# A trunk layer with its MLP on one core: another prologue, and another order at the begin of the first MLP product

## The chip, the cores and the metric

The kernel runs on one core of a Trainium2 chip, as one program. The metric is the device time of one execution in microseconds (us). A core has engines that run their own instruction queues side by side and meet only at semaphores: PE multiplies matrices, DVE and ACT work on vectors, GpSimd (POOL in the profile) too, and SP issues the DMA transfers.

## The reference, cut to what matters

One layer of a trunk over 1024 tokens of width 1024, with a context of 256 tokens:

```
m = silu(c) @ w_mod + b_mod                  # six vectors: sh1, sc1, g1, sh2, sc2, g2 (the context has two)
h = rmsnorm(x, norm1_w) * (1 + sc1) + sh1    # likewise hc of the context
proj = h @ w_in                              # q, k, v, gates, and the inputs of a short conv and a pool
mix = concat(gla(proj), conv(proj), pool(proj)) @ w_out
x = x + g1 * mix
h2 = rmsnorm(x, norm2_w) * (1 + sc2) + sh2
x = x + g2 * (square(relu(h2 @ w_mlp1)) @ w_mlp2)      # width 4096 between the two
return rmsnorm(x, final_norm_w)
```

All inputs and the output are fp32.

## The kernel before

Tensors stand transposed, 128 features to a partition block (k = 0 to 7), tokens along the free axis. A factor is split into a high part (rounded to the matrix engine's format) and a low part (what the rounding left), and a product is the sum of three: high x high, high x low, low x high. ACT makes high parts with a copy, DVE low parts with a subtraction. PE sums in PSUM, in the tiles `main`, `ob` and `sm`. Each engine's queue is written out by hand, one function per engine, and semaphores order them.

**Prologue** (to the first `gate_products`). SP loads the context, eight pieces of x, and the modulation weights `wmod` in four pieces of 2 MB, with the gate weights and the first weight tile between. ACT squares each piece over 1280 columns (1024 tokens and 256 of the context) into two accumulators and two passing buffers; DVE adds them up (`SQ_ADDED`), PE sums over the partitions, and ACT takes logarithm and exponential for the root, in two halves of the columns. `modulation_rows(j)` (L1000) multiplies one piece of `wmod` by the two vectors, eight k in `GROUPS` column groups of PE; ACT copies the rows out (`copy_rows`, L1478); `modulation_turned(j)` (L1011) turns them into columns and adds the groups up with `fold`; DVE makes shift and scale of them (`modulation`). For each k DVE scales x, ACT writes the high part, DVE the low part (`low1`, L2079). PE runs `gate_part(k)` and `value_part(k)` (L1194) on them. Before the first comes everything of pieces 0 and 1, and `low1` waits for a product of rows. `keep_busy` puts idle products of PE in the first microseconds.

**MLP1** (`h2 @ w_mlp1`). The 32 column tiles are taken in 16 pairs. Pairs 0 and 1 are plain products. From pair 2 on, the two tiles and two halves of the tokens make a 2 x 2 block product in seven products instead of eight (12 matmuls each, in the order `HID_ORDER`), for which sums of blocks are needed. Per pair:

- GpSimd makes four sums of weight blocks (`part_sums1`, L885 to L893);
- ACT makes seven high parts of weights (`w1_high`, L1826), DVE the low ones (`w1_low`, L2458);
- PE's seven products (L1382) accumulate in three banks; ACT copies them out of PSUM into `hid` (`copy_out`, L1885), DVE adds the rest (`add_out`, L2520; `third_out`), and ACT makes relu and square of the blocks (`first_out`, `next_out`, `last_block`);
- for the second MLP product the squared blocks are prepared in seven parts: DVE makes four sums (`t_made`, L2492 to L2506), ACT the high parts (`t_high`, L1880), DVE the low ones (`t_low`, L2513), all in the order `T_ORDER`, and SP stores them (`keep_hidden`, L695).

So the parts of pair i-1 are made while PE multiplies pair i. Before its copies ACT waits until all seven parts of the pair before are made (`act.wait_ge(t_lo, prev * NPART)`), since `hid` has two places. PE's products wait for the copies and sums of the pair before, whose banks they reuse (`y_copied`, `y_added`). Pairs 2 to 15 run as `period(i, ...)`, in a loop for most; the begin, with the parts of pairs 0 and 1 and pair 2, is written out. SP loads the weights for pair i+2 (`load_w1`) in the middle of the stores of pair i-1.

## Time and profile before

| | us |
|---|---|
| median of 3 runs | 1088.19 |
| lowest, highest | 1086.53, 1090.26 |
| the profiled execution | 1089.87 |
| its span, from the first to the last instruction | 1088.0 |
| PE busy | 1062.0 |
| DVE busy | 826.6 |
| ACT busy | 508.9 |
| GpSimd busy | 307.9 |

The profile is one execution. It lists the busy time of each engine, what each idle stretch ended with (the releaser), and the clock granted to PE, as a share of its full speed. Overlapping matmuls are recorded with a duration longer than their distance in time: two records of 0.39 may start 0.23 apart. The same holds for small vector instructions, of which each drains while the next starts.

### The profile page before, as it was taken

Reading aid. Unit: us, or ns where it says so; the run is one execution under the profiler, and the core shown is the slowest. Engines: PE = TensorE matmul, PEld = TensorE weight load, DVE = VectorE, ACT = ScalarE, POOL = GpSimd, SP = SyncE. Lnnn points to the kernel's source line nnn. Section 1 sums busy time; section 2 is a strip of 40 time slices with the busy share of each in tenths; the row PEclk is TensorE's granted clock in tenths of the full one; section 3 lists DMA queues with packets and bytes.
Section 4 is the critical chain, followed back from the end, with each engine's and each line's share of the span. In section 5 each row is a group of like instructions: output and inputs, shape, how many; then the busy total and the mean of one; then the engine's idle time right before and its main releaser. Section 6 shows DMA issues by size and latency. Waiting matters only on the chain.

```text
span 1088.0 us, 16279 instructions
## 1 busy us (share of the span) xinstructions
PE 1062.0 (98%) x5512; PEld 851.8 (78%) x5512; DVE 826.6 (76%) x1070; ACT 508.9 (47%) x818; POOL 307.9 (28%) x280
## 2 busy tenths in 40 slices
PE   8999999999999999998999999999999999999995
PEld 4578888777778888787888888888778888888884
DVE  4887869737544987799878787787987777777776
ACT  5657533356624312576666666666422222222234
POOL 1000006287301344013232323323333122222322
PEclk9999999999999999999999999999999999999998
DMA  9523240011013555225857566667746844864604
GB/s 369 225 97 116 89 142 31 31 40 40 21 40 136 231 191 216 78 78 227 315 229 273 232 257 245 239 262 284 295 168 259 334 185 184 339 253 185 256 1 155
DMA packets 58900, 199.80 MB, mean 184 GB/s; under 512 B 5600, under 2 KB 6880, under 8 KB 58336
## 3 DMA queue, kind: packets, MB, share of 16 engines
q1 hardware_dynamic: 58848, 199.11, 48.3%
q8 instruction: 33, 0.54, 0.2%
q14 instruction: 19, 0.16, 0.1%
HBM read 139.32 MB, written 59.77 MB: 183 GB/s over the span
## 4 chain that ended last, share of the span: by engine, by line
PE 49%; DVE 4%; issue 1%; POOL 0%; DVEq 0%; ACT 0%; ACTq 0%; POOLq 0%
PE ob L1382 13%; PE main L1424 13%; PE sm L1382 10%; PE sm L1424 8%; PE ob L1424 5%; DVE XR L2632 1%; DVE XR L2699 1%; DVE slot L2463 1%; DVE stage L2513 1%; DVE slot L2458 0%; DVE stage_last L2513 0%; DVE t_tmp L2497 0%; DVE t_tmp L2506 0%; DVE hid L2520 0%; DVE hid L2499 0%
## 5 line engine op out<-in xcount | busy, mean ns | idle before, releaser
L953 PE MATMUL main<-a_hi,w_hi 128*128 128x512 f32 x376 | 125.8, 416 | 0.0
L1382 PE MATMUL ob<-h_sum,slot 128*128 128x512 f32 x504 | 122.8, 393 | 3.0 <-DVE hid L2520 3.0
L1838 ACT ACTIVATE slot<-raw 128x512 fp32r<-128x512 f32 x80 | 50.2, 631 | 153.1 <-PE main L1424 58.4
L953 PE MATMUL main<-a_lo,w_hi 128*128 128x512 f32 x376 | 116.7, 391 | 0.0
L953 PE MATMUL main<-a_hi,w_lo 128*128 128x512 f32 x376 | 116.2, 390 | 0.0
L1382 PEld LDWEIGHTS ob<-h_sum,slot 128*128 128x128 f32 x504 | 95.7, 190 | 23.4 <-issue 3.4
L2632 DVE SCALAR_TENSOR_TENSOR XR<-main,mods,XR 128x512 f32<-128x512 f32 x112 | 83.3, 748 | 28.8 <-PE main L1424 27.7
L953 PEld LDWEIGHTS main<-a_hi,w_lo 128*128 128x128 f32 x376 | 70.6, 188 | 15.6
L953 PEld LDWEIGHTS main<-a_lo,w_hi 128*128 128x128 f32 x376 | 70.6, 188 | 15.6
L953 PEld LDWEIGHTS main<-a_hi,w_hi 128*128 128x128 f32 x376 | 66.7, 188 | 17.9 <-issue 5.8
L1424 PE MATMUL main<-t_even,slot 128*128 128x512 f32 x336 | 78.1, 389 | 0.0
L2458 DVE TENSOR_TENSOR slot<-raw,slot 128x512 fp32r<-128x512 f32 x70 | 62.5, 895 | 18.5 <-ACT slot L1826 18.5
L1382 PE MATMUL sm<-h_hi,slot 128*128 128x512 f32 x224 | 73.5, 389 | 0.0
L1424 PEld LDWEIGHTS main<-t_even,slot 128*128 128x128 f32 x336 | 63.1, 188 | 13.1
L824 POOL TENSOR_TENSOR scaled_state<-tst,decay 64x128 f32<-64x128 f32 x60 | 29.0, 483 | 151.2 <-ACT tst L1579 146.7
L2463 DVE TENSOR_TENSOR slot<-raw,slot 128x512 fp32r<-128x512 f32 x80 | 61.3, 782 | 0.2 <-ACT slot L1838 0.2
L2632 DVE SCALAR_TENSOR_TENSOR XR<-sm,mods,XR 128x512 f32<-128x512 f32 x64 | 47.7, 748 | 13.3 <-PE sm L1424 12.4
L885 POOL TENSOR_TENSOR held<-raw 128x512 f32<-128x512 f32 x14 | 24.8, 1774 | 109.7 <-DMA raw<-wstream 59.8
L914 POOL TENSOR_TENSOR raw<-part_sum,raw 128x512 f32<-128x512 f32 x16 | 21.0, 1313 | 122.3 <-DVE slot L2463 122.3
L2632 DVE SCALAR_TENSOR_TENSOR XR<-ob,mods,XR 128x512 f32<-128x512 f32 x48 | 35.8, 750 | 18.4 <-PE ob L1424 18.3
L893 POOL TENSOR_TENSOR held<-raw 128x512 f32<-128x512 f32 x14 | 23.4, 1672 | 90.9 <-DVE slot L2458 90.9
L1424 PE MATMUL main<-stage,slot 128*128 128x512 f32 x168 | 47.4, 391 | 1.5 <-DVE XR L2632 0.7
(354 smaller groups left out, 2453.7 us busy)
## 6 DMA issues: line engine op xcount, KB each, us to landing
hidden_kept<-stage SPq DMA_DIRECT2D x98, 512.0 KB, 4.2
raw<-wstream SPq DMA_DIRECT2D x60, 512.0 KB, 4.3
t_even<-hidden_kept SPq DMA_DIRECT2D x56, 512.0 KB, 5.8
raw<-wstream SPq DMA_DIRECT2D x16, 1024.0 KB, 5.2
stage<-hidden_kept SPq DMA_DIRECT2D x21, 512.0 KB, 5.4
stage_last<-hidden_kept SPq DMA_DIRECT2D x21, 512.0 KB, 6.1
wmod<-wm SPq DMA_DIRECT2D x4, 2048.0 KB, 23.6
mbuf<-wm SPq DMA_DIRECT2D x16, 512.0 KB, 4.0
```

Of the source, the lines that this page charges most:

```text
L824: pool.tensor_tensor(scaled_state[DK:P, :], tst[DK:P, h % 2, c, :], decay[DK:P, h, c:c + 1].broadcast_to([DK, DV]), ALU.mult).then_inc(sta ...
L885: pool.tensor_tensor(sums, a21, a22, ALU.add).then_inc(w1_sum, 1)
L893: pool.tensor_tensor(sums, a12, a11, ALU.subtract).then_inc(w1_sum, 1)
L914: pool.tensor_tensor(a11, sums, a11, ALU.subtract).then_inc(w2_sum, 1)
L953: ins = pe.matmul(main[:, bank, half * HALF:(half + 1) * HALF], w[:, slot, k, :], x[:, half * HALF:(half + 1) * HALF], start=begin, stop=end)
L1382: ins = pe.matmul(hid_bank(acc, odd), slots1[j][:, w, kp, :], parts[x][:, kp, :], start=PARTS[j][3] and kp == 0 and m == 0, stop=kp == KP ...
L1424: ins = pe.matmul(product_bank(s, acc, q), slots2[j][:, w, q, kp, :], tset[odd][j][kp][:, x, :], start=begins and kp == 0 and n == 0, stop ...
L1838: act.activation(slots2[j][:, 0, :, :, :], operand(s, j), ACT.Copy).then_inc(w2_hi, 1)
L2458: tt(slots1[j][:, 1, :, :], operand1(b, j), slots1[j][:, 0, :, :].bitcast(F32), ALU.subtract).then_inc(w1_lo, 1)
L2463: tt(slots2[j][:, 1, :, :, :], operand(s, j), slots2[j][:, 0, :, :, :].bitcast(F32), ALU.subtract).then_inc(w2_lo, 1)
L2513: tt(y[:, 1, :], sources(odd)[j], y[:, 0, :].bitcast(F32), ALU.subtract).then_inc(t_lo, 1)
L2632: stt(out=XR[m][:, cols], in0=product_bank(s, acc, q), scalar=mods[:, 3, m:m + 1], in1=XR[m][:, cols], op0=ALU.mult, op1=ALU.add).then_inc ...
```

## The change

**Prologue.** Each square has a buffer of its own (`square_place`), over the 1024 tokens; the squares of the context are taken once for all k and summed apart. DVE joins only squares 2 and 3, 4 and 5, and, by halves, 6 and 7. `wmod` comes in eight pieces of 1 MB, piece k when square k has been taken (they lie over the buffers of later tiles), and the rows products have 256 columns in four column groups. Modulation is done per k with two small instructions of DVE. The context is scaled early, in two instructions. Products of rows and turns for k = 2 to 7 stand between the gate and value products; the gate's high products stand ahead of its low ones. The idle products are 10 instead of 18 at the start, and two between rows(1) and turned(1).

**MLP1.** `T_ORDER` changes for all pairs but the last. In the begin, a copy out of PSUM waits for its own block's part and sum (`block_free`) instead of all seven parts of the pair before. The parts of pairs 0 to 3 stand behind weight blocks of pairs 2 to 5, in an order written out for ACT and DVE; period 5 has the rest. The part sums of pairs 2 and 3 go from GpSimd to DVE. SP loads the weights of pair 4, 5 and 6 with `load_next`, pair 4 ahead of the stores of pair 0.

The diff, cut to its core; the written orders of ACT and DVE are shown for pair 2:

```diff
-T_ORDER = (0, 3, 1, 2, 5, 4, 6)
+T_ORDER = (0, 3, 4, 1, 2, 5, 6)
 T_AT = {j: n for n, j in enumerate(T_ORDER)}
+LAST_AT = {j: n for n, j in enumerate((0, 3, 1, 2, 5, 4, 6))}
+def t_at(pair):
+    return LAST_AT if isinstance(pair, int) and pair == NMP - 1 else T_AT
...
-GROUPS = 3
+GROUPS = 4
 ROWS = 32 * GROUPS
-SHIFTED_FIRST = 3
-FILL = (18, 2)
-SQ_ADDED = (1, 2, 3, 5, 6)
-COPY_AT = {0: 1, 2: 2, 4: 3}
+FILL = (10, 2)
...
-        wmod = [at(f"wmod{j}", [P, KT, HALF], F32, HA + place * KIB) for j, place in enumerate((0, 32, 16, 48))]
+        wmod = [at(f"wmod{j}", [P, KT, 2 * P], F32, HA + (j % 2 * 32 + j // 2 * 8) * KIB) for j in range(KT)]
...
-        sq1 = at("sq1", [P, 2, NA], F32, ZA + 8 * KIB)
-        acc1 = at("acc1", [P, NA], F32, ZA + 28 * KIB)
+        squares1 = at("squares1", [P, 6, N], F32, ZA + 8 * KIB)
+        squares1_late = at("squares1_late", [P, 2, N], F32, ZT)
+        squares_c = at("squares_c", [P, KT, NC], F32, ZT + 8 * KIB)
...
             def load_wmod(j):
-                sp.dma_start(wmod[j][:, :, :].rearrange("p k c -> p (k c)"), wm1[j]).then_inc(wmod_loaded[j], 16)
+                sp.wait_ge(sq1_made, j + 1)
+                sp.dma_start(wmod[j][:, :, :], wm1[j // 2].rearrange("p (k j c) -> p k j c", j=2, c=2 * P)[:, :, j % 2, :]
+                             ).then_inc(x_wmod_loaded[j], 16)
...
             load_wmod(0)
             sp.dma_start(wg[:, :, :].rearrange("p k c -> p (k c)"), wg_in).then_inc(wg_loaded, 16)
+            load_wmod(1)
             load_tile(0)
-            load_wmod(1)
-            load_wmod(2)
-            load_wmod(3)
+            for j in range(2, KT):
+                load_wmod(j)
...
+            def load_next(i, load):
+                sp.wait_ge(w1_lo, i * NPART - NPART)
+                load()
+            load_next(2, lambda: load_w1(4, 0, stream1(4)))
             for j in T_ORDER:
                 keep_hidden(0, j)
+            for i in (3, 4):
+                for j in T_ORDER:
+                    keep_hidden(i - 2, j)
+                load_next(i, lambda: load_w1(i + 2, i % 2, stream1(i + 2)))
+            for j in T_ORDER:
...
-            part_sums1(2, 0, first=True)
-            part_sums1(3, 1)
...
-                    ins = pe.matmul(sm[32 * g:32 * g + 32, s % 2, :], silu_wide[:, k, :], wmod[j][:, k, :],
+                    ins = pe.matmul(sm[32 * g:32 * g + 32, s % 2, 0:2 * P], silu_wide[:, k, :], wmod[j][:, k, :],
...
-                for q in range(4):
+                for q in range(2):
...
+            pe.wait_ge(squares_c_added, 2)
+            for q in range(2):
+                ins = pe.matmul(ob[:, HALF:HALF + NC], ones, squares_c[:, q, :], start=q == 0, stop=q == 1)
+            ins.then_inc(sums_c_done, 1)
+            for ready, k in (((sq1_made, 1), 0), ((sq1_made, 2), 1), ((acc1_made, 1), 2), ((acc1_made, 2), 4)):
+                pe.wait_ge(*ready)
+                sums_of(square_place(k), (1, 0), k == 0, False)
+            for n, half in enumerate((1, 0)):
+                pe.wait_ge(acc1_made, 3 + n)
+                sums_of(square_place(7), (half,), False, True).then_inc(sums1_done, 1)
             modulation_rows(0)
             modulation_turned(0)
             modulation_rows(1)
+            keep_busy(FILL[1])
...
             gate_part(0)
+            modulation_rows(2)
             value_part(0)
-            modulation_rows(2)
-            gate_part(1)
             modulation_turned(2)
-            value_part(1)
-            modulation_rows(3)
-            gate_part(2)
-            value_part(2)
-            modulation_turned(3)
-            for k in range(3, KT):
+            for k in range(1, KT - 1):
+                if k + 2 < KT:
+                    modulation_rows(k + 2)
                 gate_part(k)
-                if k >= 4:
-                    value_part(k - 1)
+                if k + 2 < KT:
+                    modulation_turned(k + 2)
+                value_part(k)
+            gate_part(KT - 1)
             value_part(KT - 1)
...
-                act.wait_ge(x_loaded[k], 16)
-                if k in SQ_ADDED[2:] + (KT - 1,):
-                    act.wait_ge(acc1_made, sq_place(k) - 1)
-                act.activation(SUM_FIRST[k][:, :] if k in SUM_FIRST else sq1[:, sq_place(k) % 2, :], xs[:, k, :],
-                               ACT.Square).then_inc(sq1_made, 1)
+                act.activation(mrow[:, j % 2, :], sm[0:ROWS, s % 2, 0:2 * P], ACT.Copy).then_inc(small_free[s % 2], 1)
+            act.activation(squares_c[:, :, :], xs[:, :, N:NA], ACT.Square).then_inc(squares_c_made, 1)
...
+                act.activation(square_place(k), xs[:, k, 0:N], ACT.Square).then_inc(sq1_made, 1)
+                if k == 2:
+                    act.wait_ge(sums_c_done, 1)
+                    log1(slice(N, NA), ob[:, HALF:HALF + NC])
+                    act.wait_ge(rs1_made, 1)
+                    root1(slice(N, NA))
...
+                if k + 2 < KT:
+                    copy_rows(k + 2)
...
+            def modulation(k):
+                s = S_OF[("turn", k)]
                 dve.wait_ge(small_done, s + 1)
-                for q in range(2):
-                    i = 2 * j + q
-                    ts(ab1[:, i, 0:2], sm[:, s % 2, 4 * q:4 * q + 2], one_col("bmod", i), None, ALU.add)
-                    ins = ts(ab1[:, i, 2:4], sm[:, s % 2, 4 * q + 2:4 * q + 4], one_col("bmod", KT + i), 1.0, ALU.add, ALU.add)
-                ins.then_inc(small_free[s % 2], 1)
-                dve.wait_ge(*small_freed(s))
-                ts(ab1[:, 2 * j, 2:4], ab1[:, 2 * j, 2:4], one_col("n1", 2 * j), None, ALU.mult)
-                ts(ab1[:, 2 * j + 1, 2:4], ab1[:, 2 * j + 1, 2:4], one_col("n1", 2 * j + 1), None, ALU.mult).then_inc(ab_made, 1)
-                dve.wait_ge(ab_made, j + 1)
-            for n, k in enumerate(SQ_ADDED):
-                dve.wait_ge(sq1_made, k + 1)
-                acc = acc1 if k < 4 else acc1b
-                tt(acc[:, :], acc[:, :], sq1[:, n % 2, :], ALU.add).then_inc(acc1_made, 1)
-                dve.wait_ge(acc1_made, n + 1)
+                ts(ab1[:, k, 2:4], sm[:, s % 2, 2:4], mods[:, 0, k:k + 1], one_col("n1", k), ALU.add, ALU.mult)
+                ts(ab1[:, k, 0:2], sm[:, s % 2, 0:2], one_col("bmod", k), None, ALU.add).then_inc(small_free[s % 2], 1)
+                dve.wait_ge(*ab_ready(k))
...
+            dve.wait_ge(sq1_made, 4)
+            tt(square_place(2), square_place(2), square_place(3), ALU.add).then_inc(acc1_made, 1)
+            dve.wait_ge(rs1_made, 2)
+            scale_context(0)
+            dve.wait_ge(sq1_made, 6)
+            tt(square_place(4), square_place(4), square_place(5), ALU.add).then_inc(acc1_made, 1)
+            dve.wait_ge(sq1_made, 8)
+            for half in (1, 0):
+                cols = slice(half * HALF, (half + 1) * HALF)
+                tt(square_place(7)[:, cols], square_place(7)[:, cols], square_place(6)[:, cols], ALU.add).then_inc(acc1_made, 1)
+            scale_context(1)
...
+            for k in range(1, KT):
+                modulation(k)
+                scale1(k)
+                if k == 1:
+                    weight_low(0)
+                if k < 3:
+                    low1(k)
+                elif k > 3:
+                    low1(k - 1)
...
+            def block_free(pair, j, sums=0):
+                if sums:
+                    act.wait_ge(t_sum, pair * 4 + sums)
+                act.wait_ge(t_lo, pair * NPART + (T_AT[j] + 1))
...
             t_high(0, 0, 0, "first")
+            t_high(0, 0, 3, "first")
             w1_high(2, 0, 0, True)
             w1_high(2, 1, 0, True)
             plain_hidden(1, 0)
-            t_high(0, 0, 3, "first")
-            t_high(0, 0, 1, "first")
             w1_high(2, 2, 0, True)
-            t_high(0, 0, 2, "first")
             w1_high(2, 3, 0, True)
+            w1_high(2, 4, 0, True)
+            block_free(0, 0, 1)
+            copy_out(2, 0, 0, ACC_A, 0, 0, 0)
             plain_hidden(1, 1)
-            act.wait_ge(t_sum, 1)
-            act.wait_ge(t_lo, T_AT[0] + 1)
-            copy_out(2, 0, 0, ACC_A, 0, 0, 0)
-            w1_high(2, 4, 0, True)
-            t_high(0, 0, 5, "first")
-            t_high(0, 0, 4, "first")
-            t_high(0, 0, 6, "first")
             w1_high(2, 5, 0, True)
             w1_high(2, 6, 0, True)
-            for j in T_ORDER[:2]:
-                t_high(1, 1, j, "plain")
+            t_high(0, 0, 4, "first")
+            block_free(0, 4)
+            copy_out(2, 0, 1, ACC_A, 2, 0, 1)
+            t_high(0, 0, 1, "first")
+            t_high(0, 0, 2, "first")
+            copy_out(2, 0, 2, ACC_C, 3, 1, 1)
+            w1_high(3, 0, 1)
+            w1_high(3, 1, 1)
             first_out(2, 0)
-            act.wait_ge(t_lo, NPART)
-            copy_out(2, 0, 1, ACC_A, 2, 0, 1)
-            copy_out(2, 0, 2, ACC_C, 3, 1, 1)
+            t_high(0, 0, 5, "first")
+            next_out(2, 0)
+            t_high(0, 0, 6, "first")
...
+            def part_sums1(pair, b, steps):
+                v, sums = pair - 2, held[:, :, :]
+                a11, a12, a21, a22 = quarter1(b, 0, 0), quarter1(b, 0, 1), quarter1(b, 1, 0), quarter1(b, 1, 1)
+                for step in steps:
+                    if step == 0:
+                        dve.wait_ge(w1_loaded[b], pair * 16 + 16 * b)
+                        if v > 0:
+                            dve.wait_ge(w1_lo, v * NPART + (HID_AT[3] + 1 - NPART))
+                        ins = tt(sums, a21, a22, ALU.add)
+                    elif step == 1:
+                        dve.wait_ge(w1_sum, v * 4 + 1)
+                        ins = tt(a21, a11, a21, ALU.subtract)
+                    elif step == 2:
+                        dve.wait_ge(w1_sum, v * 4 + 2)
+                        dve.wait_ge(w1_lo, v * NPART + (HID_AT[0] + 1))
+                        ins = tt(a11, sums, a11, ALU.subtract)
+                    else:
+                        dve.wait_ge(w1_sum, v * 4 + 3)
+                        dve.wait_ge(w1_lo, v * NPART + (HID_AT[1] + 1))
+                        ins = tt(sums, a12, a11, ALU.subtract)
+                    ins.then_inc(w1_sum, 1)
...
+            part_sums1(2, 0, (0, 1))
+            w1_low(2, 0, 0)
+            part_sums1(2, 0, (2,))
+            w1_low(2, 1, 0)
+            t_made(0, 0, 1, "first")
             t_low(0, 0, 0)
-            w1_low(2, 0, 0)
-            w1_low(2, 1, 0)
+            w1_low(2, 2, 0)
+            w1_low(2, 3, 0)
             dve.wait_ge(sum_made, 13)
             sum_low(2)
+            part_sums1(2, 0, (3,))
+            w1_low(2, 4, 0)
+            t_made(0, 0, 2, "first")
+            t_made(0, 0, 3, "first")
             t_low(0, 0, 3)
-            t_low(0, 0, 1)
-            w1_low(2, 2, 0)
-            t_low(0, 0, 2)
-            w1_low(2, 3, 0)
-            t_made(0, 0, 4, "first")
-            w1_low(2, 4, 0)
-            t_low(0, 0, 5)
-            add_out(2, 0, 0, ACC_B, 1, 0, 0)
             t_low(0, 0, 4)
-            t_low(0, 0, 6)
             sum_low(3)
             w1_low(2, 5, 0)
-            for j in T_ORDER[:2]:
-                t_low(1, 1, j)
             w1_low(2, 6, 0)
-            for n in (1, 2, 3):
-                t_made(1, 1, n, "plain")
+            add_out(2, 0, 0, ACC_B, 1, 0, 0)
+            t_low(0, 0, 1)
+            t_low(0, 0, 2)
+            add_out(2, 0, 1, ACC_A, 4, 1, 1)
+            part_sums1(3, 1, (0, 1))
+            w1_low(3, 0, 1)
+            t_made(0, 0, 4, "first")
+            part_sums1(3, 1, (2,))
+            w1_low(3, 1, 1)
+            t_low(0, 0, 5)
+            t_low(0, 0, 6)
+            third_out(2, 0)
...
+                if kind == "fifth":
+                    t_low(prev, old, 0)
+                    t_low(prev, old, 3)
                 for n in (1, 2, 3):
                     t_made(prev, old, n)
                 w1_low(i, 3, odd)
-                t_low(prev, old, 1)
+                t_low(prev, old, 4)
                 add_out(i, odd, 0, ACC_B, 1, 0, 0)
                 w1_low(i, 4, odd)
+                t_low(prev, old, 1)
+                w1_low(i, 5, odd)
                 t_low(prev, old, 2)
...
+            period(5, 1, "fifth")
+            with dve.Fori(3, 7) as q:
```

## Rows read from the trace of the kernel before

**Rows 1.** The page: busy time, share of the span and instructions of each engine.

```profile
PE 1062.0 (98%) x5512; PEld 851.8 (78%) x5512; DVE 826.6 (76%) x1070; ACT 508.9 (47%) x818; POOL 307.9 (28%) x280
```

**Rows 2.** Waits of PE: line, releaser: us in total, times, longest.

```profile
PE ob L1382 <- DVE hid L2520: 3.0, 1, 3.0
```

**Rows 3.** Windows: length; busy (x) PE, PEld, DVE, ACT, POOL; clock; DMA; GB/s.

```profile
25.00:50.00 25.00, 22.95 (x129) 11.26 (x124) 21.20 (x41) 16.59 (x24) 1.51 (x3) 0.93 0.68 283
```

**Rows 4.** Timeline of ACT, squares and the last root: start, us, engine, line, operation.

```profile
9.24 1.27 ACT L1485 ACTIVATE acc<-xs 128x1280 f32<-128x1280 f32 x1 [5.79 <-DMA xs<-xt]
...
18.62 1.27 ACT L1485 ACTIVATE sq<-xs 128x1280 f32<-128x1280 f32 x1 [0.50 <-DVE acc1b L2069]
...
25.53 0.63 ACT L1499 ACTIVATE rs<-rs 128x512 f32<-128x512 f32 x1
```

**Rows 5.** Timeline of PE and DVE to the first gate product and after.

```profile
29.70 4.10 PE L1000 MATMUL sm<-wmod,silu_wide 128*32 128x512 f32 x16 [0.58 <-DMA wmod<-wm]
...
33.89 1.23 DVE L2079 TENSOR_TENSOR a_lo<-sq,a_hi 128x1024 fp32r<-128x1024 f32 x1 [2.57 <-PE sm L1000]
...
35.60 0.65 PE L1194 MATMUL main<-a_hi,wg_parts 128*64 128x512 f32 x2
...
38.61 2.77 PE L1000 MATMUL sm<-wmod,silu_wide 128*32 128x512 f32 x16
...
42.51 0.95 PE L1011 MATMUL sm<-fold,mrow 96*128 96x2 f32 x8
```

**Rows 6.** Timeline of DVE and PE at the end of the prologue.

```profile
63.70 1.22 DVE L2139 CAST zsb<-main 32x1024 fp32r<-32x1024 f32 x1 [0.79 <-PE ob L1196]
...
67.18 0.36 PE L1183 MATMUL ob<-zsb,gw_parts 128*128 128x256 f32 x1
```

**Rows 7.** Windows of 2 us: context loading, then pieces of 2 MB.

```profile
4.00:6.00 2.00, 2.00 (x5) 1.20 (x4) 1.20 (x6) 0.00 (x0) 0.60 (x2) 1.00 1.06 374
...
24.00:26.00 2.00, 2.00 (x14) 0.48 (x14) 0.97 (x2) 1.94 (x4) 1.86 (x3) 1.00 1.06 453
```

**Rows 8.** Timeline of PE, pair 2 of MLP1 and its end.

```profile
492.76 0.39 PE L1382 MATMUL ob<-h_hi,slot 128*128 128x512 f32 x1
...
500.92 2.88 PE L1382 MATMUL sm<-h_sum,slot 128*128 128x512 f32 x12
...
512.24 4.58 PE L1382 MATMUL ob<-h_sum,slot 128*128 128x512 f32 x12 [3.00 <-DVE hid L2520]
...
516.66 0.39 PE L1382 MATMUL ob<-h_hi,slot 128*128 128x512 f32 x1
```

**Rows 9.** Window of the late product and the next.

```profile
512.00:516.00 4.00, 3.76 (x10) 2.99 (x11) 4.00 (x6) 2.63 (x5) 1.60 (x1) 0.57 0.66 255
```

**Rows 10.** Timeline of DVE at the begin of MLP1.

```profile
482.56 2.29 DVE L2469 TENSOR_TENSOR h_sum<-h_raw,h_sum 128x2048 fp32r<-128x2048 f32 x1
...
484.76 0.69 DVE L2492 TENSOR_TENSOR t_tmp<-hid 128x512 f32<-128x512 f32 x1
...
504.41 1.28 DVE L2513 TENSOR_TENSOR stage<-hid,stage 128x512 fp32r<-128x512 f32 x2
...
511.42 0.67 DVE L2520 TENSOR_TENSOR hid<-hid,ob 128x512 f32<-128x512 f32 x1
...
513.22 2.37 DVE L2513 TENSOR_TENSOR stage<-hid,stage 128x512 fp32r<-128x512 f32 x2
```

**Rows 11.** Timeline of ACT and GpSimd there.

```profile
488.26 0.62 ACT L1880 ACTIVATE stage<-hid 128x512 fp32r<-128x512 f32 x1
...
504.63 3.42 POOL L885 TENSOR_TENSOR held<-raw 128x512 f32<-128x512 f32 x1 [5.90 <-DVE slot L2458]
...
512.84 1.60 POOL L890 TENSOR_TENSOR raw<-held,raw 128x512 f32<-128x512 f32 x1 [3.10 <-DVE slot L2458]
```

**Rows 12.** Timeline of DVE in a later pair.

```profile
541.44 0.69 DVE L2520 TENSOR_TENSOR hid<-hid,sm 128x512 f32<-128x512 f32 x1 [0.37 <-PE sm L1382]
...
547.93 1.64 DVE L2458 TENSOR_TENSOR slot<-raw,slot 128x512 fp32r<-128x512 f32 x1 [1.43 <-ACT slot L1826]
```

More of the change, by code:

```diff
@@ L186 @@
 BANKED = ("vt", "kt", "kc", "cs", "u", "A", "ns", "pl", "md")
-SMALL = [(_name, _j) for _j in range(KT // 2) for _name in ("rows", "turn")]
+SMALL = [(_name, _j) for _j in range(KT) for _name in ("rows", "turn")]
 for _t in range(NPROJ):
@@ L1017, in keep_busy @@
                 for _ in range(count):
[L1018 removed]
+                    pe.matmul(main[:, 0, 0:NFIRST], ones, small[:, 0:NFIRST], start=True, stop=True)
             pe.wait_ge(small_in_done, 16)
@@ L1022, in _, with sums_of @@
             pe.wait_ge(c_ready, 1)
-            def sums_of(squares, halves, with_context, first, last):
+            def sums_of(squares, halves, first, last):
                 for half in halves:
@@ L1187, in gate_products, with first_product_of @@
                 ins.then_inc(tile_done, 1)
-            def first_product_of(k, m, rows, parts):
+            def first_product_of(k, m, rows, parts, first=True, last=True):
                 for n, (w, x, c) in enumerate(parts):
-                    begin, end = k == 0 and n == 0, k == KT - 1 and n == len(parts) - 1
+                    begin, end = first and k == 0 and n == 0, last and k == KT - 1 and n == len(parts) - 1
                     for half in range(2):
@@ L1956, in period @@
                 w1_high(i, 5, odd)
-                t_high(prev, old, 4)
+                t_high(prev, old, 5)
                 copy_out(i, odd, 2, ACC_C, 3, 1, 1)
@@ new lines, in _ @@
+            third_out(3, 1)
+            w1_low(4, 1, 0)
+            w1_low(4, 2, 0)
+            t_low(2, 0, 1)
+            t_low(2, 0, 2)
+            w1_low(4, 3, 0)
+            t_made(2, 0, 4)
+            t_low(2, 0, 5)
+            add_out(4, 0, 0, ACC_B, 1, 0, 0)
+            w1_low(4, 4, 0)
+            t_low(2, 0, 6)
+            t_made(3, 1, 1)
+            t_low(3, 1, 0)
+            t_low(3, 1, 3)
+            w1_low(4, 5, 0)
+            t_made(3, 1, 2)
+            t_made(3, 1, 3)
@@ L2581, in period @@
+            t_low(3, 1, 4)
+            w1_low(4, 6, 0)
+            t_low(3, 1, 1)
+            add_out(4, 0, 1, ACC_A, 4, 1, 1)
+            w1_low(5, 0, 1)
+            t_low(3, 1, 2)
+            t_made(3, 1, 4)
+            third_out(4, 0)
+            w1_low(5, 1, 1)
+            t_low(3, 1, 5)
+            t_low(3, 1, 6)
             def period(i, odd, kind=""):
```

325 lines of the change are left out of this document (178 added, 147 removed).

## The prediction, made before the changed kernel ran

> **What bounds the kernel now.** I read the page's busy times first: the matrix engine (PE) is busy 1062.0 of the 1088.0 us span [rows 1], so what the change can give back is the other 26 us and the stretches at the lower clock. The list of PE's waits comes next. Its longest entry after the first load is one stall of 3.0 us behind DVE's sum `hid` (L2520) [rows 2], the place that the second half of the change rewrites. The windows of 25 us then show the one other weak stretch, the prologue: from 25 to 50 us PE is busy 22.95 of 25 and its clock is granted 0.93 [rows 3]. Then I went through the timeline of both stretches. Nearly everything behind each of them is PE's own queue, so a microsecond won or lost there should reach the end of the kernel.
>
> **The prologue, before.** Eight squares of 1280 columns take ACT from 9.24 to 19.89 (18.62 + 1.27), each waiting for a 512 KB piece of x or for DVE; then sums, logarithms, and the last root, done at 26.16 [rows 4]. But the first gate product starts only at 35.60, because `a_lo` waits (2.57 us) for the second product of modulation rows, which itself waited 0.58 us for its 2 MB of `wmod` and ran 4.10 instead of 2.77 us [rows 5]. From 35.60 to `gate_products` at 67.18 [rows 6] are 31.6 us.
>
> **The prologue, after.** *Squares.* With a buffer for each square ACT waits only for x. I let the last piece land near 18.0: the first square starts at 9.24, and seven further pieces at the 374 GB/s of 4 to 6 us [rows 7] would take 9.8 us, but the old last square, which waited 0.50 for DVE [rows 4], puts the last one at 18.1 or before. Its square over 1024 columns takes 1.0 to 1.1 (1.27 x 0.8), DVE adds two halves, 0.6 each (1.23 for 1024 columns [rows 5], halved), PE sums two halves (0.9 each, estimated as half of four recorded matmuls), done at 21.1 and 22.0. Logarithm and root per half (about 0.65 each with the root's 0.63 [rows 4]) end at 23.9 instead of 26.16.
>
> *First gate product.* Rows(0) now has 256 columns in four column groups instead of 512 in three. The trace holds no such product: half of 2.77 [rows 5] is 1.39 if groups do not help, and 1.04 if they share in proportion (3/4). I take 1.1, nearer the second, since the parts of one product in the trace overlap already. A turn falls from 8 recorded matmuls in 0.95 [rows 5] to four, 0.45. So: rows(0) at 22.0, turn at 23.8 (it waits for the copy on DVE), rows(1) at 24.3, two fillers 1.4, turn(1) at 26.7, gate(0) at 27.2. That is 8.4 us ahead of 35.60.
>
> *The loop.* Six rows products and turns that stood before 35.60, or beside it, now stand between the gate and value products: 6 x (1.1 + 0.45) = 9.3. The eight gate and value parts: 2.72 us for 12 matmuls of 512 columns [rows 8] is 0.23 each, half that for 256, so gate 4 x 0.23 + 2 x 0.12 = 1.16, value 6 x 0.23 + 3 x 0.12 = 1.74, together 8 x 2.9 = 23.2. DVE has some 3.0 us per k (scale 1.2, low part 1.2, context 0.34, small ones 0.26) beside PE's 4.5, ACT 2.5, so both are covered; I add 1.2 for the first two k, where they are not ahead yet. 27.2 + 23.2 + 9.3 + 1.2 = 60.9 is the end of the last value product. The copies for the gates start 1.7 before (59.2) and take 3.3 (before: 63.70 to 67.18, 3.48, of it some on PE's last word [rows 6]): `gate_products` at 62.5, 4.7 us before the old 67.18. PE then stands 1.6 us, and a stall of 3 us cost clock in this trace [rows 9]; I leave 0.5 for that: **-4.2 us**.
>
> *Bounds.* The eight 1 MB pieces of `wmod` are read in runs of 1 KB. The context, in such runs too, moves at 374 GB/s at the start, where the 2 MB pieces later move at 453 [rows 7]; I took 353, a little under the low one, so that a piece lands every 3 us, with the gate weights and the first weight tile between at 21, 24, 29, 32, 35, 38, 41 and 44 us, each ahead of its product. At 294 GB/s `gate_products` comes at 65.0, and at 252 at 67.7, past the old. Rows products of 1.39 instead of 1.1 give 64.5. At the upper rate and 1.0 us a product it is 61.6. So -5.6 to about 0, the value nearer the good end. The Trainium skill (DMA: Bandwidth & Descriptors, the specification table) puts the full line rate at transfers from 512 B up; by that rule the 1 KB runs would cost nothing, and an estimate with it is 0.3 us earlier. The slower windows stand at the start of the kernel, so they do not decide it.
>
> **MLP1's begin, before.** PE starts pair 2 at 492.76, three products later is at 500.92 (2.72 each), and so is due for the seventh at 509.08; it starts it at 512.24 and the next at 516.66 [rows 8]. 3.16 us late, and 4.42 - 2.72 = 1.70 more in a product that ran at a granted clock of 0.57 [rows 9]: the old loss is **4.86 us**. The cause is DVE's queue, full from 484.76 until the sum at 511.42 [rows 10].
>
> **MLP1's begin, after.** The freed copies let ACT go ahead, and the parts of the plain pairs are spread behind the weight blocks. But DVE does no less: it takes over eight part sums from GpSimd (pairs 2 and 3), and the work that was crowded before 512 is moved to pairs 3, 4 and 5. So I ask when DVE reaches the last sum that PE needs before the steady state, add_out(5,1). From 484.77 to it, in the order written out, DVE has 106 instructions:
> 101 of 128x512 (28 weight low parts, 34 hidden low parts, 20 sums for parts, 11 add_out, 8 part sums). Two in a row take 1.28 with 0.68 for one [rows 10], a pitch of 0.60: 60.6.
> 2 low parts of 128x2048 at 2.20 (482.56 to 484.76 [rows 10]) and 3 third_out at 0.64: 6.3.
> GpSimd: an instruction of DVE beside one of GpSimd takes longer. Two hidden low parts took 2.37 at 513.22, 1.28 at 504.41 [rows 10], beside a GpSimd sum of 1.60 [rows 11]: 1.09 held. In the new order GpSimd still does pairs 4, 5 and 6, ten sums in this stretch: 9 x 1.1 + 0.3 = 10.2. Add_out has an operand in PSUM and stayed at 0.67 and 0.69 [rows 10, 12], so I charge it nothing.
> Waits of DVE for ACT and PE, by adding ACT's queue at 0.62 for a copy [rows 11] beside it: 2.6 before the first weight block, since ACT must first make t_high(0,3), at 488.26 before as well; 1.6 in the rest of pair 2, 0.9 for PE's fifth product, 1.5 in pair 3, 1.5 in pair 4, 2.6 in pair 5, 1.1 for DVE's own semaphores: 11.8.
> Sum 88.9: add_out(5,1) is done at 573.7. PE is due there after 27 products, at 492.76 + 27 x 2.72 = 566.2. PE is late by 7.5 us in all, in pieces: about 1.9 in pair 3, 0.8 and 1.7 in pair 4, 0.7, 1.5 and 1.0 in pair 5. The old piece of 3.16 is gone, and what is late next is the same queue, one to three pairs later. No piece reaches 3 us, so I take no loss of clock. One sum of GpSimd in the old trace, 3.42 long instead of 1.60 [rows 11], waited itself instead of holding DVE; one of the ten so gives 0.5 back: **7.0, against 4.86: +2.1 us.**
> *Bounds.* The holds decide. Without any, DVE's work is 10.2 shorter, its waits for ACT grow in the place of most of that slack, and what stays late is 0.8: -4.1. At 1.2 a hold it is 8.6: +3.8. The queue of SP costs nothing: the load for pair 4 is moved ahead of the stores, and its buffer is free as early as before; the seven stores that now stand behind it free places of parts that ACT needs one pair later.
> By the Trainium skill (SBUF — State Buffer, "SBUF: two separate sides"), an instruction of DVE with two SBUF inputs and one of GpSimd that reads SBUF exclude each other for the whole instruction. The trace agrees in kind, since add_out with its PSUM operand is not held, and not in size: 1.09 of 1.60.
>
> **The sum.** -4.2 + 2.1 = -2.1. The profiled execution took 1089.87 (span 1088.0 and 1.87 around it) and would take 1087.8; it lies 1.68 above the median of 1088.19, against which the forecast is **1086.1**.
>
> **The rivals.**
> *B, the stalls vanish.* DVE's instructions and GpSimd's fall into each other's gaps: in the steady pairs before, one of four sums held DVE (547.93, 1.64 [rows 12]). With two of ten holds the late sum is 1.5 or less: -3.4, and with -4.2: 1080.6. For it speaks that DVE now has less crowding at any one time; against it, that DVE stays nearly without idle time to 574.
> *C, the prologue gives less than it says.* Rows products cost 1.39 or the pieces of `wmod` come late, so `gate_products` is at 64.5: -2.7, and with +2.1 the time is 1087.6. For it: the product that followed late data ran 4.10 [rows 5]. Against: the pieces are half as large and the first one is asked for a good 8 us before its use.
> *D, slower: the holds recur in every pair.* In the steady state after pair 5 DVE has 22 instructions, 13.2 us, in a pair of 19.04 (7 x 2.72), and four sums of GpSimd beside them. At 1.1 a hold that is 17.6 at most, and the pair fits with a few tenths left once waits are counted. From about 1.3 a hold it does not, and each of the ten pairs 6 to 15 pays: at 1.4 it is 0.7 a pair, 7.3, and 12.8 at the begin, +7.9 + 7.3 - 4.2 = +11; just past the point +5, so 1093 to 1099, and I take 1093 as its time. For it: the order inside the periods is changed, so the gaps that GpSimd found before [rows 12] are not the same. Against: no hold of one instruction above 1.1 in the trace. The skill's rule above, with its whole instruction (1.60), would bring this case for certain: an estimate by it is 17 us at the begin and 1.5 a pair.
>
> **How the numbers follow.** Forecast 0.50, with its own range of 1083.5 to 1089; B 0.28; C 0.10; D 0.12. A measurement of this kernel can tell about 0.3%, 3.3 us, from no change: the border is at 1084.9 and 1091.5. Faster: B's 0.28 and 0.14 of the forecast's 0.50 make 0.42. Same: 0.36 and C's 0.10 make 0.46. Slower: D, 0.12. The range goes from B's time with the prologue's bound less one, 1079.5, to 1091.5, short of D.
>
> **What would show it.** Right: `gate_products` near 62.5 with the first gate product near 27; no PE stall near 512, and several of 0.7 to 2 us between 525 and 575, released by DVE or ACT; DVE without idle time there, with instructions of 1.6 to 1.7 beside GpSimd's. Wrong: rows products over 1.3 us or waits for `wmod`; PE without stalls from 520 to 575; or a wait for L2520 or L1885 in every later pair.

## The result, and the profile after

The changed kernel takes 1091.16 us (median of 20 runs, 1089.54 to 1092.85) against 1088.1 for the kernel before, taken beside it: 1.0026 times as long, with a 95% interval of 1.0020 to 1.0033. I had forecast 1086.1, two microseconds faster. The time lies inside the range, but on the other side of no change. The profiled execution took 1092.85 (span 1091.1), the slowest of the 20.

The prologue did nearly what was forecast. Timeline of PE in the changed kernel (columns as in [rows 5, 6]):

```profile
24.45 1.07 PE L1016 MATMUL sm<-wmod,silu_wide 128*32 128x256 f32 x16
...
27.16 0.65 PE L1210 MATMUL main<-a_hi,wg_parts 128*64 128x512 f32 x2
...
63.14 0.36 PE L1199 MATMUL ob<-zsb,gw_parts 128*128 128x256 f32 x1 [1.80 <-DVE zsb L2229]
```

A product of rows takes 1.07 (forecast 1.1), the first gate product starts at 27.16 (27.2; before 35.60), `gate_products` at 63.14 (62.5; before 67.18): 4.04 us earlier. But PE stood 1.80 us ahead of it, and behind it the clock fell. Windows of the changed kernel (columns as in [rows 3]):

```profile
62.00:64.00 2.00, 0.86 (x5) 0.81 (x6) 0.75 (x3) 1.50 (x3) 0.00 (x0) 1.00 1.02 377
64.00:66.00 2.00, 2.00 (x14) 2.00 (x13) 2.00 (x3) 0.30 (x1) 0.00 (x0) 0.66 0.55 211
66.00:68.00 2.00, 2.00 (x11) 2.00 (x10) 1.61 (x2) 1.91 (x3) 0.00 (x0) 0.50 0.27 59
...
475.00:500.00 25.00, 25.00 (x112) 20.70 (x111) 20.94 (x24) 17.55 (x22) 0.00 (x0) 1.00 0.23 85
500.00:525.00 25.00, 25.00 (x112) 20.72 (x111) 22.85 (x35) 17.67 (x32) 3.31 (x2) 1.00 0.77 294
525.00:550.00 25.00, 21.64 (x88) 17.10 (x86) 22.84 (x32) 14.47 (x26) 6.63 (x4) 0.93 0.65 234
550.00:575.00 25.00, 22.19 (x94) 17.47 (x95) 22.32 (x29) 16.26 (x30) 7.97 (x5) 1.00 0.86 318
```

The first product of pair 2 starts at 490.20, only 2.56 us earlier than before [rows 8]: 1.5 went to the half clock (the lower of 1.2 and 2.4 GHz) between 64 and 68. The lower four windows are MLP1's begin. PE, whose loss at 500 to 525 was 3 us before, is full there now, and loses 3.4 and 2.8 us in the two windows behind it. Timeline of PE in the changed kernel, the late products and the ones that follow:

```profile
490.20 0.39 PE L1405 MATMUL ob<-h_hi,slot 128*128 128x512 f32 x1
...
527.73 4.48 PE L1405 MATMUL ob<-h_sum,slot 128*128 128x512 f32 x12 [2.01 <-DVE hid L2629]
...
532.01 0.51 PE L1405 MATMUL ob<-h_hi,slot 128*128 128x512 f32 x1
...
550.12 2.97 PE L1405 MATMUL ob<-h_sum,slot 128*128 128x512 f32 x12 [1.48 <-DVE hid L2629]
...
561.89 3.01 PE L1405 MATMUL sm<-h_sum,slot 128*128 128x512 f32 x12 [0.64 <-DVE slot L2544]
...
566.15 3.04 PE L1405 MATMUL ob<-h_sum,slot 128*128 128x512 f32 x12 [1.25 <-ACT hid L1914]
...
572.70 3.00 PE L1405 MATMUL ob<-h_sum,slot 128*128 128x512 f32 x12 [0.80 <-DVE hid L2629]
...
575.54 0.39 PE L1405 MATMUL ob<-h_hi,slot 128*128 128x512 f32 x1
```

575.54 is the first product of pair 6, 28 products after 490.20; at 2.72 each it would be at 566.36. So 9.2 us are lost (before: 4.86): 6.2 are the waits in brackets, 1.6 the product at 527.73, which took 4.28 instead of 2.72 at the lower clock, the rest some tenths after each wait. The waits stand where the forecast put them, and DVE is what is late. Its own waits, from 482 to 573 us (line, releaser: us, times, longest):

```profile
DVE slot L2544 <- ACT slot L1855: 5.4, 5, 1.8
DVE stage L2622 <- ACT stage L1909: 3.3, 5, 1.2
DVE held L2555 <- DMA raw<-wstream: 0.7, 1, 0.7
DVE hid L2629 <- PE ob L1405: 0.7, 1, 0.7
```

These are 10.1 us (forecast 11.8). The kernel before had no such wait from 484 to 512. Of these waits 4.6 us lie before 512. And where GpSimd begins its sums, DVE is held, so that its instruction ends only after GpSimd's (timeline of GpSimd and DVE):

```profile
521.03 1.68 POOL L903 TENSOR_TENSOR held<-raw 128x512 f32<-128x512 f32 x1 [98.22 <-DVE slot L2544]
521.47 1.79 DVE L2544 TENSOR_TENSOR slot<-raw,slot 128x512 fp32r<-128x512 f32 x1
...
523.18 1.78 DVE L2622 TENSOR_TENSOR stage<-hid,stage 128x512 fp32r<-128x512 f32 x1
```

1.79 instead of 0.69, the hold of 1.1 that I had read from [rows 10, 11]. Of the ten sums of GpSimd from 521 to 573 us nine held DVE so. The Trainium skill (SBUF — State Buffer, "SBUF: two separate sides") lets the one that starts first keep the other out for its whole instruction. The sum of 1.68 was 0.44 us old when DVE's instruction began, so 1.24 of it were left, against a hold of 1.1: the trace agrees with the rule in size too, to 0.14 us. The prediction had denied that, since it compared the hold with the whole 1.60.

At the end the kernel loses another 0.9 us: from ACT's last instruction to the end of the span it is 6.6, before 5.6 (below).

### The profile page after: what moved, and what is told of

Same layout as the page of the kernel before. It is cut to its first block, busy times and chain, and to the rows that moved or that the text cites. A ratio compares the mean times of both kernels' runs of the same rounds, so it can differ in the third digit from the quotient of the medians.

```text
span 1091.1 us, 16343 instructions
## 1 busy us (share of the span) xinstructions
PE 1059.0 (97%) x5566; PEld 851.3 (78%) x5566; DVE 845.1 (77%) x1070; ACT 511.9 (47%) x827; POOL 297.0 (27%) x272
## 4 chain that ended last, share of the span: by engine, by line
PE 75%; DVE 12%; issue 4%; ACT 4%; POOL 3%; DMA 1%; DVEq 0%; SPq 0%; ACTq 0%; POOLq 0%
PE main L969 17%; PE main L1447 13%; PE ob L1405 11%; PE sm L1447 8%; PE sm L1405 7%; PE ob L1447 6%; PE main L987 2%; PE main L1338 2%; DVE stage L2622 1%; POOL scaled_state L843 1%; POOL tst L846 1%; PE main L1210 1%; PE main L1371 1%; PE ob L1371 1%; PE ob L1003 1%
## 5 line engine op out<-in xcount | busy, mean ns | idle before, releaser
L903 POOL TENSOR_TENSOR held<-raw 128x512 f32<-128x512 f32 x12 | 20.1, 1672 | 142.3 <-DVE slot L2544 142.3
L1405 PEld LDWEIGHTS sm<-h_hi,slot 128*128 128x128 f32 x224 | 42.0, 188 | 8.7
```

The costliest lines, as they stand in the source:

```text
L1405: ins = pe.matmul(hid_bank(acc, odd), slots1[j][:, w, kp, :], parts[x][:, kp, :], start=PARTS[j][3] and kp == 0 and m == 0, stop=kp == KP ...
```

## The experiments

Each ran beside the kernel before; the ratio is to its runs, with the 95% interval. MLP1 is the stretch from the first product of pair 2 to the first of the second MLP product, in the profile: 271.8 us before, 276.5 in the changed kernel.

**1 and 2: each half alone.** No edit but leaving out the other half's.

> The changed prologue with the MLP1 of the kernel before. Theory (clock): gate_products comes 4.0 us earlier, but PE stands 1.8 us before it and the matmuls behind it run at half clock for 1.5 us more; net -2.5, so 1085.6 against 1088.1. Rival (the loss of 3 us is in the prologue: later tiles lose what the prologue won): 1088 to 1091. What I had forecast for this part: -4.2, 1083.9.

1085.38 us, 0.9985 (0.9976 to 0.9994), against 1087.67 for the kernel before beside it: the time that the theory gave, but its reason is not in the profile, so that the agreement is in part luck. `gate_products` comes at 63.17 after the same stall, and the clock does not fall, neither there nor at the old stall of 3.0 us in MLP1:

```profile
508.33 2.99 PE L1392 MATMUL ob<-h_sum,slot 128*128 128x512 f32 x12 [2.99 <-DVE hid L2540]
511.16 0.39 PE L1392 MATMUL ob<-h_hi,slot 128*128 128x512 f32 x1
```

The product behind the stall takes 2.83 us here; in [rows 8] it took 4.42.

> The prologue of the kernel before with the changed MLP1. Theory: the begin of MLP1 loses 9.2 us instead of 4.9, and the change to MLP2 0.4 more: +4.7, so 1092.8 against 1088.1. Rival (the two halves disturb each other, MLP1 alone is as forecast): +2.1, 1090.2. Rival (the end of the kernel, where the profiled execution shows 0.9 us more from the last instruction to the last store, is part of the change): +5.6, 1093.7.

1092.56 us, 1.0040 (1.0027 to 1.0054), 4.9 above the same 1087.67: the whole loss, and more, is MLP1's. The rival with the end does not hold, since the end is 5.6 us here, as in the kernel before. The clock stays at 1.00 behind the longest stall:

```profile
530.53 2.97 PE L1395 MATMUL ob<-h_sum,slot 128*128 128x512 f32 x12 [1.87 <-DVE hid L2609]
533.34 0.39 PE L1395 MATMUL ob<-h_hi,slot 128*128 128x512 f32 x1
```

MLP1 takes 275.0 us against 270.7 in experiment 1: 4.3 us longer with no fall of the clock in either. Its begin loses 7.7 us (pair 6 starts at 576.85, 28 products after 493.00) against 3.8.

**3: is it the clock?**

```diff
             value_part(KT - 1)
+            pe.wait_ge(*ab_ready(KT - 1))
+            for _ in range(2):
+                pe.matmul(sm[:, 0, 0:NFIRST], ones, small[:, 0:NFIRST], start=True, stop=True)
             gate_products(0)
...
                     if j == 6:
+                        if nth == 2:
+                            pe.wait_ge(plain_relu, 4)
+                            for _ in range(2):
+                                pe.matmul(main[:, 0, 0:NFIRST], ones, small[:, 0:NFIRST], start=True, stop=True)
```

> The changed kernel, with two idle products of PE ahead of gate_products and two ahead of the wait of the last product of pair 3; no other work changes. Theory (clock): PE no longer stands 1.80 and 2.17 us there, the clock stays at 1.00, and 1.5 + 1.6 us come back: 1088.1 against 1091.2. Rival (the slow products are due to something else, weight loads or PSUM): 1091.2, or up to 0.5 slower where an idle product ends after the wait.

1090.57 us, 1.0030 (1.0018 to 1.0042): not what the theory said. In its profile the clock stays at 1.00 in both places, the two waits are 0.6 and 0.7, and that execution (1090.0) is 2.9 below the profiled one of the changed kernel. But the medians do not differ: the changed kernel's profile had been its slowest execution, and three of the six runs here have a mean clock of 0.994 as well. Of ten profiles with the 1.8 us stall unfilled, three show the fall behind it. So the clock's price in a profile is a draw, and it does not explain the 3 us. It may hold a part of them: the mean clock is 0.9946 over the 20 runs of the changed kernel and 0.9954 over 68 of the kernel before, and 0.0008 of 1090 us is 0.9 us, an estimate of the most that this can be.

**4: are the holds real?** GpSimd's sums shortened:

```diff
-                sums = held[:, :, :]
+                cut = lambda a: a[:, 0:1, 0:1]
+                a11, a12, a21, a22, sums = cut(a11), cut(a12), cut(a21), cut(a22), cut(held[:, :, :])
```

> The changed kernel with the part sums of GpSimd (pairs 4 to 15) cut to one column of 512, so that GpSimd hardly holds DVE; these sums are left out of the computation. Theory (holds): the ten holds of 1.1 us before add_out(5,1) go, the late pieces of pairs 3 to 5 shrink from 9.2 us to 1 or 2, and the kernel takes 1083 to 1084. Rival (DVE's eight added sums and the waits for ACT in the written order make it late, not the holds): 1089 to 1091.

1083.62 us, 0.9966 (0.9953 to 0.9979): 7.5 below the changed kernel, as the holds ask. The short sums are also ready earlier, which this run can't tell from the holds; experiment 5 leaves nothing out. All that is left of PE's waits from 484 to 760 us, in MLP1 and at the step to the second product:

```profile
PE sm L1406 <- DVE slot L2545: 0.6, 1, 0.6
PE main L1448 <- DVE stage_last L2623: 0.6, 1, 0.6
PE ob L1406 <- ACT hid L1915: 0.2, 1, 0.2
```

**5: all sums on DVE in the changed kernel.** `part_sums1` of pairs 4 to 15 in DVE's periods (steps 0 to 2 behind `w1_low(i + 1, 0)`, step 3 behind `w1_low(i, 3)`), none on GpSimd.

> The changed kernel with the part sums of all pairs on DVE, none on GpSimd; nothing is left out. Theory (holds): up to add_out(5,1) DVE gets ten more instructions of 0.60 (6.0 us) and loses the holds of 10.2, so PE is late by about 4.0 instead of 6.7 us: 1088.4 against 1091.2. Rival (DVE's own work is what counts, and holds hide in its waits): ten instructions later, 1094 to 1097, and a wait in every later pair.

1086.53 us, 0.9985 (0.9976 to 0.9994): 4.6 below the changed kernel, more than I said. MLP1 takes 271.9. Four more instructions of DVE in a pair (2.4 us) cost less than four of GpSimd beside it. Without any hold the changed order is still 3.2 us behind the old one (experiment 6).

**6, 8 and 11: the old order, with the sums on DVE.** The changed prologue, the order of MLP1 before, and (11: for pairs 2 and 3 only, GpSimd the rest):

```diff
             sum_low(1)
+            part_sums1(2, 0, (0, 1))
             for n in (1, 2, 3):
                 t_made(0, 0, n, "first")
             t_low(0, 0, 0)
             w1_low(2, 0, 0)
+            part_sums1(2, 0, (2,))
...
             w1_low(2, 3, 0)
+            part_sums1(2, 0, (3,))
...
             w1_low(3, 0, 1)
+            part_sums1(3, 1, (0, 1))
...
             w1_low(3, 1, 1)
+            part_sums1(3, 1, (2,))
```

> The changed prologue, the order of MLP1 of the kernel before, and the part sums of all pairs on DVE (four of pair 2 before the late sum, those of pair 3 behind it). Theory (holds): before add_out(2,1) six holds of 1.1 go (6.4 us) and four instructions of 0.60 come, so the stall of 3.0 us goes and some 1.2 us of small waits in pair 3 are left; against the prologue alone (1085.4) about -2: 1083.3. Rival (the stall comes from the copies that wait for all seven parts, which the change frees): the stall stays at 2 to 3 us, 1085 to 1086. Rival (the steady pairs have no room for four more instructions on DVE): 1090 or more.

1083.34 us, 0.9948 (0.9934 to 0.9962), as the theory says; both rivals fail. The stall of 3 us is gone; MLP1 takes 268.5. Waits of PE from 484 to 760:

```profile
PE sm L1368 <- DVE slot L2454: 0.5, 1, 0.5
PE main L1410 <- DVE stage_last L2532: 0.2, 1, 0.2
PE ob L1368 <- ACT hid L1877: 0.2, 1, 0.2
```

> The changed prologue, the old order of MLP1, and only the part sums of pairs 2 and 3 on DVE; GpSimd makes those of pairs 4 to 15. Theory (the holds count only in the crowded stretch before 512): as with all sums on DVE, 1083.3. Rival (holds in pairs 4 to 6 make it late there): 1085 or more.

1084.15 us, 0.9968 (0.9957 to 0.9979), MLP1 269.4, between the theory and the rival: 0.8 us above experiment 6, which the intervals leave open. This kernel and the changed one have the same prologue and the same instructions on DVE and GpSimd in MLP1. They differ in the written order (with `T_ORDER`, the freed copies and the load ahead of the stores), and together these cost 7.0 us between the medians; between profiles without a fall of the clock it is 5.6 to 6.0 us of MLP1 (experiments 2, 3 and 7 against this one). Windows of this kernel:

```profile
475.00:500.00 25.00, 25.00 (x112) 20.68 (x111) 24.06 (x29) 19.89 (x28) 0.00 (x0) 1.00 0.60 231
500.00:525.00 25.00, 23.97 (x103) 18.67 (x102) 23.90 (x37) 15.93 (x30) 3.30 (x2) 1.00 0.79 294
525.00:550.00 25.00, 24.87 (x110) 20.32 (x109) 21.78 (x33) 17.31 (x31) 8.01 (x5) 1.00 0.73 269
```

DVE is busy 24.06 and 23.90 us in the first two windows, 20.94 and 22.85 in the changed kernel: 4.2 us more is done by 525, while GpSimd hardly works and holds nobody (this kernel's pair 2 starts 1.8 us earlier, at 488.40, which is a part of it). The old order does not wait less in all, it waits later. Of DVE's waits to 575 us, 9.1 here and 10.1 in the changed kernel, 0.8 lie before 525 here and 6.0 there. The rest of them here, from 525 to 575, when PE hardly waits any more:

```profile
DVE slot L2475 <- ACT slot L1839: 6.7, 6, 1.4
DVE hid L2560 <- PE sm L1389: 1.6, 5, 0.4
```

> The kernel with the changed prologue, the old order of MLP1 and all part sums on DVE, with two idle products of PE ahead of gate_products. Theory (the clock falls after a stall in some executions only): the stall of 1.8 us becomes 0.6, and the mean gain is a part of 1.5 us: 0.3 to 1.0 below the same kernel without them, about 1082.6. Rival (the clock there is no matter of the stall): no difference.

1083.25 us, 0.9950 (0.9936 to 0.9963): 0.1 below experiment 6. The wait ahead of `gate_products` became 0.6, and the time did not move; both profiles have the clock at 1.00 there. Whether the idle products help on average can't be told from five runs.

**7: sums of pairs 2 and 3 back on GpSimd** in the changed kernel.

> The changed kernel with the part sums of pairs 2 and 3 back on GpSimd, as in the kernel before. Theory (holds cost more than the instructions they replace, but DVE has waits for ACT in pair 2 that take them up): PE is late as much as before, within 0.5 us of the changed kernel: 1091.2. Rival (each of the eight holds costs 0.5 more than DVE's own instruction, all on the path): +4, 1095.

1091.53 us, 1.0028 (1.0018 to 1.0037): no difference, as forecast, but not quite for the reason given. Two of the eight sums fall into a wait of DVE for ACT (4.0 us, to 484.50); the other six hold it for 6.0 us in all, against 4.8 us of the instructions that they replace.

**9: ACT's first weight blocks first.** `t_high(0, 0, 3)` moved behind `w1_high(2, 1)`.

> The changed kernel with one instruction of ACT moved: the high part (0,3) comes behind the first two weight blocks of pair 2 instead of ahead of them, so DVE's first wait of 2.2 us shrinks. Theory (DVE's early waits are not on the path by themselves: it then waits for PE's fifth product at 506 instead; what is lost is that parts of pairs 0 and 1 stand behind the weight blocks of pairs 3 to 5): 1091.2, unchanged. Rival (this wait, the first in my list, is what makes DVE late): 2 us less, 1089.

1090.6 us, 1.0021 (1.0012 to 1.0030): no difference. DVE no longer waits for the first weight block, but for the fourth it then waits 2.22 instead of 1.02 us, because ACT waits there for the plain product of PE that frees the block's place. DVE's waits add up to 10.2, as before.

**10: the freed copies alone**, in experiment 1's kernel.

```diff
-            act.wait_ge(t_lo, NPART)
+            act.wait_ge(t_lo, T_AT[4] + 1)
             copy_out(2, 0, 1, ACC_A, 2, 0, 1)
```

> The changed prologue with the old order of MLP1, where the second copy out of PSUM of pair 2 waits for its own block's part instead of all seven: the freed copies alone. Theory (holds and DVE's queue): the stall of 3.0 us stays, 1085.4 as with the prologue alone. Rival (the wait for all parts is what delays DVE's sum): the stall shrinks by 1 us or more, 1083.5 to 1084.5.

1085.98 us, 0.9979 (0.9969 to 0.9989), the stall is 3.1 us: the wait for all seven parts was not what made DVE's sum late. The edit alone would be a weak test, since in the old `T_ORDER` block 4's part is the sixth of the seven. But in experiment 1 this copy already came right behind ACT's instruction before it, without a wait, so no earlier release could have helped:

```profile
498.14 0.58 ACT L1901 ACTIVATE hid<-ob 128x512 f32<-128x512 f32 x1
```

Here the clock fell behind the stall, and the late product took 4.11 us:

```profile
510.44 4.31 PE L1392 MATMUL ob<-h_sum,slot 128*128 128x512 f32 x12 [3.12 <-DVE hid L2540]
514.55 0.63 PE L1392 MATMUL ob<-h_hi,slot 128*128 128x512 f32 x1
```

**12 and 13: the end of the kernel.** 12 is the kernel before with each piece of `wmod` in two transfers of runs of 1 KB; 13 is experiment 6 with the array laid out so that the eight pieces are contiguous.

> The kernel before, with each of the four pieces of wmod loaded by two transfers of 1 MB in runs of 1 KB. Question: in every profile with the changed prologue the kernel ends 6.5 us after ACT's last instruction, in every one without it 5.65; and what do the short runs cost. Theory (the 0.85 us come with the smaller DMA packets): 6.5 here too. Rival (they come with the rest of the prologue's program): 5.65. Runs of 1 KB at a lower rate would also make the second product of rows wait for its data by some us longer than 0.58.

1093.03 us, 1.0053 (1.0035 to 1.0070). PE waits 2.8 instead of 0.6 us for the second piece, and the end is the long one, as the theory said; but this run has eight transfers as well as short runs.

> The kernel with the changed prologue, the old order of MLP1 and all part sums on DVE (1083.3), with the array of modulation weights laid out so that each of the eight 1 MB pieces is contiguous, 8 KB for a partition instead of eight runs of 1 KB. Theory (the 0.85 us after the last byte come with the number of small packets, not with the number of transfers, which stays eight): the kernel ends 5.65 us after ACT's last instruction, the pieces move at 450 instead of 349 GB/s, and the time is 0.8 to 1.0 lower, 1082.4. Rival (the number of transfers or the waits of SP's queue make the longer end): 6.5 us, 1083.3.

1084.1 us, 0.9961 (0.9947 to 0.9974): not faster than experiment 6, and the end stays long, so the rival holds. The pieces move at 424 GB/s, not 450. ACT's last instruction in the kernel before (span 1088.0), in experiment 6 (1081.6), 12 (1089.7) and 13 (1083.6):

```profile
1081.65 0.72 ACT L2015 ACTIVATE XR<-XR,small 128x512 f32<-128x512 f32 x1 [0.51 <-POOL XR L936]
```

```profile
1074.36 0.72 ACT L2007 ACTIVATE XR<-XR,small 128x512 f32<-128x512 f32 x1 [0.51 <-POOL XR L915]
```

```profile
1082.53 0.72 ACT L2017 ACTIVATE XR<-XR,small 128x512 f32<-128x512 f32 x1 [0.51 <-POOL XR L938]
```

```profile
1076.37 0.72 ACT L2006 ACTIVATE XR<-XR,small 128x512 f32<-128x512 f32 x1 [0.50 <-POOL XR L914]
```

From its end to the span's: 5.6, 6.5, 6.5 and 6.5 us. The short end goes with four transfers of `wmod` (the kernel before and experiment 2), the long one with eight, with short runs or without, in the old prologue (12) or the new. Why four transfers at the start move the last store's completion by 0.9 us was not found.

## Why the prediction was wrong, point by point

- **What bounds the kernel** was right: both halves of the change work on PE's queue, and what they won or lost there reached the end, but for 0.9 us that are lost behind PE's last work.
- **The prologue, -4.2.** The terms held: last square at 17.87 (18.0), root done at 23.70 (23.9), products 1.07 (1.1), `gate_products` 0.6 later than summed, since `a_lo` of k = 6 came 0.6 late and the gate tile with it. `wmod` came at 347 GB/s (353 taken) and was never waited for. What I left out is the end: 0.9 us for eight transfers, which the sum puts at nothing. The 4.0 us won, less these and the 0.5 for the clock (a fall of 1.5 in three of ten profiles), make -2.6; experiment 1 measures -2.3 between the medians, and by its ratio -1.6.
- **MLP1's stalls, 7.0.** Right in cause, place and size: 6.2 us of waits where I had 7.6 before the half microsecond taken off, in pairs 3, 4 and 5, four released by DVE and one by ACT; a hold of 1.1; DVE's waits 10.1 instead of 11.8. In experiment 2, where the clock does not fall, pair 6 starts 7.7 us late. Experiment 4 takes the holds away and 7.5 us go.
- **The step that failed** is the one after it: "7.0, against 4.86: +2.1 us". The old 4.86 is 3.16 of stall and 1.70 of lower clock, and I entered the clock as a sure loss of the old kernel. It is not: the same stall of 3 us costs 0.1 in experiment 1 and 1.4 in experiment 10 (4.11 for the product behind it). For the new stalls I wrote "No piece reaches 3 us, so I take no loss of clock"; a stall of 2.01 lost 1.6 in the changed kernel and one of 2.00 lost 1.7 in experiment 9, those of 1.87 and 2.15 in experiments 2 and 7 nothing. Compared stall with stall, my own terms give 7.0 - 3.16 = +3.8, and profiles without a fall in MLP1 give 275.0 - 270.7 = +4.3 (0.4 of it at the step to the second product, where the last pair is late by as much). The median of experiment 2 is +4.9. The sum had a sign of it: I noted that the profiled execution lies 1.68 above the median, and took the 1.70 of clock off the median all the same. No span of 68 further runs of the kernel before is longer than that profile's 1088.0 (1084.0 to 1088.0, median 1086.0). Whether the 1.68 are the same microseconds is not shown.
- **Sum.** -2.3 and +4.9 make +2.6; measured are +3.1, within what the intervals leave open.
- **The rivals.** B needed GpSimd's sums to find gaps: one of the ten did, the one that I had allowed for. C did not happen as described: rows and `wmod` were as taken. D did not happen: behind 575.54 PE does not wait in MLP1; 1.1 a hold leaves room in the steady pair, as I worked out. The estimate of 17 us in D took the whole 1.60 of a sum as held; the trace holds DVE for what is left of it, 1.1.
- **What I could have seen.** I noted 11.8 us of waits of DVE in the new order and none in the old, took them as given, and asked only how late DVE would be. The question that pays is when they come, and what DVE could do in them: the parts of pairs 0 and 1, which the old order makes there. Experiment 11 has the same instructions in the old order and is 7.0 us faster. That the moved sums are not at fault is shown by experiments 7 and 11. The written order, the new `T_ORDER`, the freed copies and the load ahead of the stores were not parted: experiment 10 frees one copy in the old order only. I wrote that SP's queue costs nothing; ACT waits for stores in the new order (1.0 us in the changed kernel, 2.2 in experiment 2) and not in experiment 11, and whether that reaches PE is not known.

## What to carry to other kernels

Where an engine has work for all the time it is given, an order that lets it idle early and moves work later loses what it idled, even if its waits are no longer in all: count its busy time up to the point where slack begins. Price a stall by its length, and the clock behind it as a chance, the same for old and new; one profile shows one draw. When two engines hold each other, price the work on both: four sums a pair take DVE 2.4 us, and up to 4.4 us of holds when GpSimd makes them; on DVE and in the old order they remove the stall (1083.3 us in experiments 6 and 8, the fastest here, 0.995 of the kernel before).

## What the runs showed of the hardware that I had not expected

- The same stall of PE, 3.0 us at the same instruction, was followed by a granted clock of 0.50 to 0.71 in two profiles (the kernel before and experiment 10, windows of 2 us) and by 1.00 in another (experiment 1); a stall of 1.8 us by a fall in three of ten, one of 1.9 to 2.2 us in MLP1 by a fall in two of five.
- With four more transfers near its start the kernel's end is 0.8 to 0.9 us longer, whatever the size of their runs: 6.5 or 6.6 us in 13 profiles of 13, against 5.6 in two of two.
- `wmod` in runs of 1 KB came at 347 GB/s, the same bytes in runs of 8 KB at 424, each with the DMA engines full. The window of the changed kernel, then that of experiment 13 (the last column is GB/s):

```profile
28.00:32.00 4.00, 3.92 (x32) 2.55 (x30) 3.59 (x6) 2.65 (x5) 0.00 (x0) 1.00 1.10 347
```

```profile
28.00:32.00 4.00, 4.00 (x33) 2.45 (x32) 3.73 (x6) 2.79 (x5) 0.00 (x0) 1.00 1.03 424
```

  The Trainium skill (DMA: Bandwidth & Descriptors, the specification table) has the full rate from 512 B up; here runs of 1 KB fall short of 8 KB by 18%. Nothing waited for them.
